# A two-layer transformer stack on one core: in the first feed-forward layer, half a plain column block moves to right behind the first pair's last product

## The chip, the cores and the metric

The kernel runs on one core of one Trainium2 chip. The metric is the time of one execution on the device in microseconds (us), here the median of several runs. Engines are called TensorE (PE), VectorE (DVE), ScalarE (ACT), GpSimd (POOL) and SyncE (SP).

## What is computed

256 tokens of width 1024 go through one layer of a first model (feed-forward, mixer of neighbourhood attention and pooling, feed-forward, a gated embedding) and two layers of a second model (feed-forward, mixer, feed-forward each). The change touches only the very first feed-forward layer, `f1`:

```python
D_MODEL = 1024; SEQ = 256; D_FF = 2816

def rms_norm(x, g):
    xf = x.astype(jnp.float32)
    y = xf * lax.rsqrt(jnp.mean(xf * xf, axis=-1, keepdims=True) + RMS_EPS)
    return (y * g.astype(jnp.float32)).astype(x.dtype)

def swiglu(x, w_gate, w_up, w_down):
    return (jax.nn.silu(x @ w_gate) * (x @ w_up)) @ w_down
...
        f = swiglu(rms_norm(h, ffn1_pre_g[i]), ffn1_w_gate[i], ffn1_w_up[i], ffn1_w_down[i])
        h = h + 0.5 * rms_norm(f, ffn1_post_g[i])
```

## The kernel before

**Tiles.** All products are float32-accurate and are made of three fp32r products: high part of the tokens with high part of the weight, low with high, high with low. A weight tile is 512 rows (four blocks of 128) by 512 columns, 1 MB, and comes in one DMA into a buffer `wholeN`. ScalarE copies it into a buffer `splitM` in fp32r (the **high part**, line 1554, counted by `act_hi`), and VectorE subtracts (the **low part**, line 2029, counted by `dve_lo`, written to `splitN`, over the place of the raw tile). TensorE then runs 12 matmuls of 512 columns for each of the two token tiles `t` = 0, 1: four with the high part (line 892), four with the tokens' low part (line 896), four with the weight's low part (line 905).

**Plain blocks and pairs.** The gate and up projections have 11 column blocks (256 gate columns and the 256 up columns beside them). Blocks 0 to 4, 9 and 10 of `f1` are **plain**: `("tile", j, n)` is block j with rows n of 0, 1, 24 matmuls for both token tiles, into `bank0` and `bank1` or `bank2` and `bank3`. Blocks (5, 6) and (7, 8) are **pairs**: instead of eight block products (two column blocks, two halves of the rows, two token tiles) there are seven, of 12 matmuls each (lines 954, 956, 959), on sums of weights and of tokens, as in Strassen's scheme: `b11`, `t1`, `t2`, `b22`, `t3`, `b21`, `t4`. They share `bank6` and `bank7`, and ScalarE and VectorE carry results between them in the working tiles `u1`, `u2`, `s5`, `c4`, which all lie in `xn`. For a second pair (`g` = 1):

- `b11` goes to `bank6` and must wait until the first pair's `t4` has been read out of it: ScalarE's gate (line 1690) and then VectorE's multiplication (line 2303, the wait on `mult` of the pair's first block).
- ScalarE then copies `bank6` to `u1` (line 1713). This copy waits for `turn 5`, since `turn 5` still reads the old `u1`. Product `t2`, which accumulates into `bank6`, waits for that copy (`fn.of("u1", name, g)`).
- The raw weights of `t1` and `t3` are sums that GpSimd makes with an accumulating DMA (line 704) on top of a first load. Those of `t2` and `t4` are sums that VectorE makes (line 2033): `t2` from `b22` and `t1`; `t4` from `b21` and `t2`.

**Turns.** `("turn", j)` is four transposes on TensorE (line 842) of a finished block of the hidden layer; ScalarE takes the high part (line 1559, `th`), VectorE the low part (line 2076, `tl`).

**What sets the order.** One table, `LATE_PAIRS` (lines 27 to 39), lists tiles, turns and products. Every engine's program for `f1` walks this table, and the number of a weight tile in the plan (`spot`) is its place in it. SyncE issues the loads in the order of `load_key`, which follows the plan's number, with the weights of `t1` pulled to just ahead of `b11`. ScalarE and VectorE also work ahead. At a table's step with weight i, before what else the step asks of it, ScalarE makes the high parts of all weights up to `ahead(i, 1)`, in order, and VectorE the low parts up to `behind(i)`:

```python
        def ahead(i, gap=2):
            j = i
            while j + 1 < NT and j < i + 5 and needed[j + 1] <= i - gap:
                j += 1
            return j
        def behind(i):
            return max(i, ahead(i, 1) - 1)
                elif step == "product":
                    act_high(act, ahead(spot[(name, *what)], 1))
                    product(*what)
```

`needed[j]` is the last weight whose buffers tile j takes over. Each engine works strictly in its own order, so whatever stands behind a waiting instruction waits too. The plan before numbers the weights around the change: 18 is `t4` of the first pair, 19 `b11` of the second, 20 `tile 10, 0`, 21 `t1`, 22 `t2`, 23 `tile 10, 1`, 24 `b22`, 25 `t3`, 26 `b21`, 27 `t4`.

Of the kernel before, what the change touches and what calls it, by code (L numbers as in the profile page):

```python
# [31 lines left out]
    ("product", 0, "b11"), ("tile", 4, 1),  # L32
    ("product", 0, "t1"), ("product", 0, "t2"), ("tile", 9, 0), ("turn", 4),
    ("product", 0, "b22"), ("product", 0, "t3"), ("tile", 9, 1),
    ("product", 0, "b21"), ("product", 0, "t4"), ("turn", 6),
    ("product", 1, "b11"), ("turn", 5), ("tile", 10, 0),
    ("product", 1, "t1"), ("product", 1, "t2"), ("tile", 10, 1),
    ("product", 1, "b22"), ("product", 1, "t3"), ("turn", 9),
    ("product", 1, "b21"), ("turn", 10), ("product", 1, "t4"))
# [2828 lines left out]
```

## Time and profile before

| | us |
|---|---|
| median of 3 runs | 1577.14 |
| lowest, highest | 1576.97, 1578.09 |
| the profiled execution, whole time | 1576.5 |
| its span in the trace | 1574.7 |
| TensorE busy | 1564.3 (99% of the span) |
| VectorE busy | 1225.4 (78%) |
| ScalarE busy | 919.2 (58%) |

The profiled execution is 0.6 us shorter than the median and 1.8 us longer than its own span. TensorE is busy nearly all of the time, so the time is TensorE's work plus the few places where it waits. The changed stretch lies between 93 and 114 us from the span's start, in the third of the profile's 40 slices.

### The profile page before, as it was taken

How to read it: one execution, taken by the hardware profiler on the slowest of the kernel's cores; microseconds unless marked ns; L12 is line 12 of the kernel's file. 1: busy time of each engine (PE TensorE's matmuls, PEld its weight loads, DVE VectorE, ACT ScalarE, POOL GpSimd, SP SyncE). 2: the span in 40 equal slices, each digit the busy share in tenths (PEclk: the TensorE clock that was granted, in tenths of full speed). 3: DMA queues.
4: the chain of work that ended last, by engine and by line, in shares of the span. 5: the costliest groups of instructions: out<-in, count | busy, mean ns of one | idle time of the engine just before them, and what ended most of it. 6: DMA issues, size and time to landing. Idle time of an engine off the chain costs nothing.

```text
span 1574.7 us, 18788 instructions
## 1 busy us (share of the span) xinstructions
PE 1564.3 (99%) x7587; PEld 1303.4 (83%) x7587; DVE 1225.4 (78%) x1168; ACT 919.2 (58%) x957; POOL 116.9 (7%) x138
## 2 busy tenths in 40 slices
PE   9999999999999999999999999999999999999998
PEld 6878897788888888888988888888888998888886
DVE  6888466677889779888658898878897657688887
ACT  7556456656675776654655575466654435455752
POOL 1115000000000000001010000000000131000000
PEclk9999999999999999999999999999999999999999
DMA  9896464467876687674648777868775544576773
GB/s 347 263 272 240 161 237 144 147 244 225 273 247 233 236 285 256 213 242 181 241 161 293 211 244 218 325 209 290 241 267 206 191 170 149 194 279 210 255 219 134
DMA packets 54484, 360.25 MB, mean 229 GB/s; under 512 B 6528, under 2 KB 6912, under 8 KB 13696
## 3 DMA queue, kind: packets, MB, share of 16 engines
q1 hardware_dynamic: 44864, 308.24, 52.0%
q0 software_dynamic: 9312, 50.70, 14.5%
q8 instruction: 60, 0.98, 0.3%
q14 instruction: 24, 0.20, 0.0%
q10 hardware_dynamic: 224, 0.14, 0.0%
HBM read 358.00 MB, written 1.05 MB: 228 GB/s over the span
## 4 chain that ended last, share of the span: by engine, by line
PE 98%; DVE 1%; DMA 0%; issue 0%; ACT 0%; SPq 0%; DVEq 0%; ACTq 0%
PE bank L892 22%; PE bank L905 22%; PE bank L896 19%; PE bank L959 7%; PE bank L954 7%; PE bank L956 7%; PE bank L842 3%; PE bank L909 3%; PE bank L988 2%; PE bank L990 2%; PE bank L991 2%; DVE split L2029 0%; DMA whole<-in_w_f_gate_up 0%; PE bank L1436 0%; PE bank L1226 0%; DVE whole L2033 0%
## 5 line engine op out<-in xcount | busy, mean ns | idle before, releaser
L2029 DVE TENSOR_TENSOR split<-whole,split 128x2048 fp32r<-128x2048 f32 (+2 forms) x346 | 741.8, 2168 | 113.5 <-ACT split L1554 112.6
L1554 ACT ACTIVATE split<-whole 128x2048 fp32r<-128x2048 f32 (+1 forms) x331 | 615.6, 1879 | 235.1 <-DVE whole L2033 59.8
L892 PE MATMUL bank<-split,xh 128*128 128x512 f32 x1020 | 279.6, 396 | 0.0
L905 PE MATMUL bank<-split,xh 128*128 128x512 f32 x1020 | 273.6, 390 | 0.0
L896 PE MATMUL bank<-split,xl 128*128 128x512 f32 x848 | 227.2, 390 | 0.0
L905 PEld LDWEIGHTS bank<-split,xh 128*128 128x128 f32 x1020 | 191.1, 188 | 40.8 <-DVE split L2029 0.6
L892 PEld LDWEIGHTS bank<-split,xh 128*128 128x128 f32 x1020 | 186.8, 188 | 39.4 <-issue 3.0
L896 PEld LDWEIGHTS bank<-split,xl 128*128 128x128 f32 x848 | 159.2, 188 | 34.2
L892 PE MATMUL bank<-split,th 128*128 128x512 f32 x364 | 101.0, 394 | 0.0
L896 PE MATMUL bank<-split,tl 128*128 128x512 f32 x364 | 99.4, 389 | 0.0
L905 PE MATMUL bank<-split,th 128*128 128x512 f32 x364 | 99.4, 389 | 0.0
L896 PEld LDWEIGHTS bank<-split,tl 128*128 128x128 f32 x364 | 68.3, 188 | 14.4
L905 PEld LDWEIGHTS bank<-split,th 128*128 128x128 f32 x364 | 68.3, 188 | 14.4
L892 PEld LDWEIGHTS bank<-split,th 128*128 128x128 f32 x364 | 67.1, 188 | 13.0
L2033 DVE TENSOR_TENSOR whole<-whole 128x2048 f32<-128x2048 f32 x34 | 77.6, 2284 | 0.0
L988 PE MATMUL bank<-xh,split 128*128 128x256 f32 x256 | 72.6, 284 | 0.0
L990 PE MATMUL bank<-xl,split 128*128 128x256 f32 x256 | 72.4, 283 | 0.0
L991 PE MATMUL bank<-xh,split 128*128 128x256 f32 x256 | 72.4, 283 | 0.0
L954 PE MATMUL bank<-split,xh 128*128 128x512 f32 x224 | 61.4, 396 | 0.6 <-DVE xn L2303 0.6
L2076 DVE TENSOR_TENSOR tl<-bank,th 128x512 fp32r<-128x512 f32 x66 | 45.4, 687 | 20.8 <-ACT th L1559 20.2
L956 PE MATMUL bank<-split,xl 128*128 128x512 f32 x224 | 60.0, 390 | 0.0
L959 PE MATMUL bank<-split,xh 128*128 128x512 f32 x224 | 60.0, 390 | 0.0
(335 smaller groups left out, 1998.5 us busy)
## 6 DMA issues: line engine op xcount, KB each, us to landing
whole<-in_w_a_gate_up SPq DMA_DIRECT2D x48, 1024.0 KB, 6.9
whole<-in_w_b_gate_up SPq DMA_DIRECT2D x48, 1024.0 KB, 6.9
whole<-in_w_f_gate_up SPq DMA_DIRECT2D x46, 1024.0 KB, 8.2
whole<-in_w_ret SPq DMA_DIRECT2D x24, 1024.0 KB, 4.8
whole<-in_w_a_down SPq DMA_DIRECT2D x22, 1024.0 KB, 6.8
whole<-in_w_b_down SPq DMA_DIRECT2D x22, 1024.0 KB, 6.8
whole<-in_w_f_down SPq DMA_DIRECT2D x21, 1024.0 KB, 4.9
whole<-in_w_mix SPq DMA_DIRECT2D x16, 1024.0 KB, 4.9
```

What stands on the lines that cost most here:

```text
L892: pe.matmul(o[:, :], tokens(0, k), whi[:, k, :], start=start and k == 0, stop=False, skip_group_check=True)
L896: pe.matmul(o[:, :], tokens(1, k), whi[:, k, :], start=False, stop=False, skip_group_check=True)
L905: ins = pe.matmul(o[:, :], tokens(0, k), wlo[:, k, :], start=False, stop=end, skip_group_check=True)
L954: pe.matmul(o[:, :], xh_of(k), whi[:, k, :], start=start and k == 0, stop=False, skip_group_check=True)
L956: pe.matmul(o[:, :], xl_of(k), whi[:, k, :], start=False, stop=False, skip_group_check=True)
L959: ins = pe.matmul(o[:, :], xh_of(k), wlo[:, k, :], start=False, stop=k == 3, skip_group_check=True)
L988: pe.matmul(o, whi[:, k, cols], xh[:, k0 + k, :], start=start and k == 0 and c % 2 == 0, stop=False, skip_group_check=True)
L990: pe.matmul(o, whi[:, k, cols], xl[:, k0 + k, :], start=False, stop=False, skip_group_check=True)
L991: ins = pe.matmul(o, wlo[:, k, cols], xh[:, k0 + k, :], start=False, stop=end, skip_group_check=True)
L1554: act.activation(split[s][:, 0:n], whole[r][:, 0:n], ACT.Copy).then_inc(hi.mark(i), 1)
L2029: dve.tensor_tensor(split[r][:, c0:c1], whole[r][:, c0:c1], split[s][:, c0:c1].bitcast(F32), ALU.subtract).then_inc(lo.mark(*what), 1)
L2033: dve.tensor_tensor(whole[load_to[i]][:, :], whole[load_to[a]][:, :], whole[load_to[b]][:, :], ALU.add).then_inc(vec.mark("sum", i), 1)
```

## The change

One entry of the table moves: `tile 10, 0` (block 10 with the first half of the rows) stood behind `turn 5`, and now stands right behind the first pair's `t4`, ahead of `turn 6`. The second pair's `b11`, `turn 5` and `t1` now follow each other directly.

```diff
     ("product", 0, "b22"), ("product", 0, "t3"), ("tile", 9, 1),
-    ("product", 0, "b21"), ("product", 0, "t4"), ("turn", 6),
-    ("product", 1, "b11"), ("turn", 5), ("tile", 10, 0),
+    ("product", 0, "b21"), ("product", 0, "t4"), ("tile", 10, 0), ("turn", 6),
+    ("product", 1, "b11"), ("turn", 5),
     ("product", 1, "t1"), ("product", 1, "t2"), ("tile", 10, 1),
```

`tile 10, 0` becomes weight 19 and `b11` weight 20. No instruction is added or removed; buffers are dealt out anew from weight 17 to 29.

**TensorE**, from the first pair's `t4` (the first row) to the second pair's `t1` (the last row, with `sh`). Before:

```order
L959 MATMUL bank<-split,xh 128x512 x4
L842 MATMUL bank<-ident,xn 128x128 x4
L954 MATMUL bank<-split,xh 128x512 x4
L956 MATMUL bank<-split,xl 128x512 x4
L959 MATMUL bank<-split,xh 128x512 x4
L842 MATMUL bank<-ident,xn 128x128 x4
L892 MATMUL bank<-split,xh 128x512 x4
L896 MATMUL bank<-split,xl 128x512 x4
L905 MATMUL bank<-split,xh 128x512 x4
L892 MATMUL bank<-split,xh 128x512 x4
L896 MATMUL bank<-split,xl 128x512 x4
L905 MATMUL bank<-split,xh 128x512 x4
```

Now, from the first matmuls of `tile 10, 0` on:

```order
L892 MATMUL bank<-split,xh 128x512 x4
L896 MATMUL bank<-split,xl 128x512 x4
L905 MATMUL bank<-split,xh 128x512 x4
L842 MATMUL bank<-ident,xn 128x128 x4
L954 MATMUL bank<-split,xh 128x512 x4
L956 MATMUL bank<-split,xl 128x512 x4
L959 MATMUL bank<-split,xh 128x512 x4
L842 MATMUL bank<-ident,xn 128x128 x4
L954 MATMUL bank<-split,sh 128x512 x4
```

The 24 matmuls of lines 892 to 905 moved from behind the second turn to ahead of the first.

**ScalarE**, the same place. Line 1690 is the gate of the first pair's `t4`, `th0<-bank5` is `turn 6`, `th0<-bank4` is `turn 5`, line 1713 is the copy to `u1`; of line 1554, the one that waits for `dma_sum_t1` is weight 21 (`t1`), the one with `dve_vec` is 22 (`t2`), the one with `dma_raw9` is 23 (`tile 10, 1`). Before:

```order
L1690 ACTIVATE xn<-bank6,st 128x256 [waits pe_passed]
L1559 ACTIVATE th0<-bank5 128x512 [waits pe_turned]
L1554 ACTIVATE split8<-whole4 128x2048 [waits pe_passed,dma_sum_t1]
L1713 ACTIVATE xn<-bank6 128x512 [waits pe_turned,pe_passed]
L1559 ACTIVATE th0<-bank4 128x512 [waits pe_turned]
L1554 ACTIVATE split6<-whole0 128x2048 [waits pe_passed,dve_vec]
L1554 ACTIVATE split5<-whole9 128x2048 [waits pe_passed,dma_raw9]
```

Now:

```order
L1690 ACTIVATE xn<-bank6,st 128x256 [waits pe_passed]
L1554 ACTIVATE split4<-whole5 128x2048 [waits pe_passed,dma_sum_t1]
L1559 ACTIVATE th0<-bank5 128x512 [waits pe_turned]
L1554 ACTIVATE split6<-whole0 128x2048 [waits pe_passed,dve_vec]
L1554 ACTIVATE split8<-whole9 128x2048 [waits pe_passed,dma_raw9]
L1713 ACTIVATE xn<-bank6 128x512 [waits pe_turned,pe_passed]
L1559 ACTIVATE th0<-bank4 128x512 [waits pe_turned]
```

The copy to `u1` (line 1713) stood ahead of the high parts of 22 and 23, and stands behind them now: at its step, `b11`, the rule `ahead(i, 1)` now gives 23, where it gave 21.

**VectorE**, the same place. `tl0<-bank5` is `turn 6`, `tl0<-bank4` is `turn 5`, line 2033 makes the weight sums of `t2` and `t4`; the rows of line 2029 behind them are the low parts of `t1` and `t2`. Before:

```order
L2076 TENSOR_TENSOR tl0<-bank5,th0 128x512 [waits act_turn_hi]
L2029 TENSOR_TENSOR split1<-whole1,split3 128x2048 [waits act_hi]
L2076 TENSOR_TENSOR tl0<-bank4,th0 128x512 [waits act_turn_hi]
L2033 TENSOR_TENSOR whole0<-whole10,whole4 128x2048 [waits dma_sum_t1,dma_raw10,pe_passed]
L2029 TENSOR_TENSOR split4<-whole4,split8 128x2048 [waits act_hi]
L2033 TENSOR_TENSOR whole2<-whole11,whole0 128x2048 [waits dve_vec,dma_raw11,pe_passed]
L2029 TENSOR_TENSOR split0<-whole0,split6 128x2048 [waits act_hi]
```

Now:

```order
L2029 TENSOR_TENSOR split1<-whole1,split3 128x2048 [waits act_hi]
L2076 TENSOR_TENSOR tl0<-bank5,th0 128x512 [waits act_turn_hi]
L2033 TENSOR_TENSOR whole0<-whole10,whole5 128x2048 [waits dma_sum_t1,dma_raw10,pe_passed]
L2029 TENSOR_TENSOR split5<-whole5,split4 128x2048 [waits act_hi]
L2033 TENSOR_TENSOR whole2<-whole11,whole0 128x2048 [waits dve_vec,dma_raw11,pe_passed]
L2029 TENSOR_TENSOR split0<-whole0,split6 128x2048 [waits act_hi]
L2076 TENSOR_TENSOR tl0<-bank4,th0 128x512 [waits act_turn_hi]
```

The chain of weight sums and low parts stood behind `turn 5` and stands behind `turn 6` now.

SyncE's loads keep their number and places; only what the first of them bring is exchanged: the load that follows the first pair's `t2` brings weight 19 (`tile 10, 0`) where it brought the first part of 21 (`t1`), the load behind `tile 9, 0` brings 21 where it brought `b11`, and the load behind `b22` brings `b11` where it brought `tile 10, 0`.

## Rows read from the trace of the kernel before

**Rows 1.** The profile's page, part 1: busy time of each engine.

```profile
PE 1564.3 (99%) x7587; PEld 1303.4 (83%) x7587; DVE 1225.4 (78%) x1168; ACT 919.2 (58%) x957; POOL 116.9 (7%) x138
```

**Rows 2.** TensorE's waits, whole span: for whom, us in total, times, longest.

```profile
PE bank L959 <- DVE split L2029: 0.7, 1, 0.7
```

**Rows 3.** TensorE in order of time, 94 to 114 us: start, us, what, idle before it.

```profile
96.50 0.60 PE L842 MATMUL bank<-ident,xn 128*128 128x128 f32 x4
97.75 1.19 PE L954 MATMUL bank<-split,xh 128*128 128x512 f32 x4 [0.65 <-DVE xn L2303]
...
100.61 0.60 PE L842 MATMUL bank<-ident,xn 128*128 128x128 f32 x4
100.96 1.18 PE L892 MATMUL bank<-split,xh 128*128 128x512 f32 x4
...
106.53 1.07 PE L954 MATMUL bank<-split,sh 128*128 128x512 f32 x4
...
109.25 1.07 PE L954 MATMUL bank<-split,sh 128*128 128x512 f32 x4
...
111.97 1.20 PE L959 MATMUL bank<-split,sh 128*128 128x512 f32 x4 [0.74 <-DVE split L2029]
113.01 1.08 PE L892 MATMUL bank<-split,xh 128*128 128x512 f32 x4
```

**Rows 4.** ScalarE in order of time, the same stretch.

```profile
97.78 1.92 ACT L1554 ACTIVATE split<-whole 128x2048 fp32r<-128x2048 f32 x1
101.30 0.60 ACT L1713 ACTIVATE xn<-bank 128x512 f32<-128x512 f32 x1 [1.61 <-PE bank L842]
101.80 0.59 ACT L1559 ACTIVATE th<-bank 128x512 fp32r<-128x512 f32 x1
105.35 1.92 ACT L1554 ACTIVATE split<-whole 128x2048 fp32r<-128x2048 f32 x1 [2.96 <-DVE whole L2033]
109.96 3.72 ACT L1554 ACTIVATE split<-whole 128x2048 fp32r<-128x2048 f32 x2 [2.69 <-DMA whole<-in_w_f_gate_up]
```

**Rows 5.** VectorE in order of time, the same stretch.

```profile
102.42 0.69 DVE L2076 TENSOR_TENSOR tl<-bank,th 128x512 fp32r<-128x512 f32 x1 [1.76 <-ACT th L1559]
103.03 2.28 DVE L2033 TENSOR_TENSOR whole<-whole 128x2048 f32<-128x2048 f32 x1
105.23 2.29 DVE L2029 TENSOR_TENSOR split<-whole,split 128x2048 fp32r<-128x2048 f32 x1
107.43 2.28 DVE L2033 TENSOR_TENSOR whole<-whole 128x2048 f32<-128x2048 f32 x1
109.63 6.77 DVE L2029 TENSOR_TENSOR split<-whole,split 128x2048 fp32r<-128x2048 f32 x3
```

**Rows 6.** Line 650, SyncE's weight loads, 93 to 95 us: issue, issue to landing.

```profile
L650 SPq DMA_DIRECT2D whole<-in_w_f_gate_up x1: 328/328/328, 94.0 to 94.0; - x1
...
DMA to landing us min/median/max: 16.0/16.0/16.0
```

**Rows 7.** The same line, 79 to 81 us.

```profile
L650 SPq DMA_DIRECT2D whole<-in_w_f_gate_up x1: 328/328/328, 79.9 to 79.9; - x1
...
DMA to landing us min/median/max: 6.3/6.3/6.3
```

**Rows 8.** Line 704, GpSimd's accumulating load, 83 to 84 us.

```profile
L704 POOL DMA_DIRECT2D whole<-in_w_f_gate_up x1: 983/983/983, 83.4 to 83.4; - x1
...
DMA to landing us min/median/max: 14.3/14.3/14.3
```

**Rows 9.** Stretches: us, busy PE, PEld, DVE, ACT, POOL, clock, DMA share, GB/s.

```profile
94.00:106.00 12.00, 11.35 (x54) 9.21 (x53) 10.16 (x9) 5.20 (x7) 1.37 (x2) 1.00 1.03 331
```

**Rows 10.** DMA packets, 89 to 96 us: packets, MB, share of 16 engines.

```profile
q0 software_dynamic: 128, 0.99, 67.9%
q1 hardware_dynamic: 132, 0.95, 34.2%
```

**Rows 11.** TensorE's first matmuls of the span.

```profile
1.20 3.53 PE L1514 MATMUL bank<-junk 128*128 128x512 bf16 x8 [1.20 <-DVE eps L2721]
```

## The prediction

> **What bounds the kernel now.** I read the page first: TensorE is busy 1564.3 of 1574.7 us [rows 1], so only its work and its few waits set the end. No work is added or taken away here, so I looked at its waits. Outside the kernel's first 7 us, the view of waits has two, and both lie in the changed stretch: one for a weight's low part [rows 2] and one for VectorE's multiplication, which stands as idle time in the order of time [rows 3]. I then read the three engines in order of time over that stretch [rows 3 to 5], and last the DMAs that feed it [rows 6 to 10].
>
> The reader is to see two things in rows 3. Four matmuls of 512 columns take 0.907 us, since the 12 of `t1` take from 106.53 to 109.25, 2.72 us. And two steps take longer. (a) `turn 6` starts at 96.50 and its successor `b11` at 97.75, 1.25 us where `turn 5` and its successor need 0.35 (100.61 to 100.96): 0.90 us lost, waiting for the first pair's last multiplication. (b) `t2` takes 3.76 us (109.25 to 113.01) where 2.72 are due: 1.04 us lost, waiting for its low part. Together 1.94 us, 0.12% of the time. This is all that the move can give back.
>
> **The change, part by part: TensorE.** `t4` ends at 96.50, and nothing up to there is touched on TensorE. `tile 10, 0` now starts there. Its high part is made where ScalarE made that of `b11`, its low part likewise; both are older than 96.50 or end before it is needed. Cost 24 matmuls, 6 x 0.907 = 5.44 us, to 101.94, as before but earlier. The wait (a) goes: the multiplication was done at 97.7. Then `turn 6` 0.35, `b11` 2.72, plus 0.13 that the first matmuls behind a turn always cost (97.75 to 100.61 is 2.86 [rows 3]): 105.14. `turn 5` 0.35 brings `t1` to 105.49, where before it stood at 106.53. So far the gain is 1.04 us.
>
> **The change: VectorE.** Its chain (sum for `t2`, low part of `t1`, sum for `t4`, low part of `t2`; 2.2 us each) started at 103.03, right behind `turn 5`'s low part, for which it had waited on ScalarE [rows 5]. Now it stands behind `turn 6`, and that turn starts at 101.94. From `turn 5` at 100.61 [rows 3] to the chain at 103.03 were 2.42 us, of which ScalarE's copy to `u1` held up nothing more than 0.50 (101.30 to 101.80 [rows 4]). Without that copy the chain starts at 101.94 + 1.92 = 103.86, so 0.83 later than before, for products that TensorE wants 1.04 earlier. The low part of `t1` ends at 107.43 + 0.83 = 108.26. TensorE wants it at 105.49 + 0.13 + 1.81 = 107.43, gets it at about 108.4, and ends `t1` at 109.44. The low part of `t2` ended at 111.83 (109.63 + 2.2) and ends at 112.66.
>
> **The change: ScalarE, the step that decides.** The copy to `u1` (line 1713) ran at 101.30 [rows 4] as soon as `turn 5` was through, eight us before `t2` needed it. Now ahead of it stand the high parts of weights 22 and 23. That of 22 waits for VectorE's sum and ended at 107.15; it shifts with the chain to 108.0. That of 23 (`tile 10, 1`) waits for a load which was issued at 94.0 and took 16.0 us [rows 6]: ScalarE began it at 109.96 after 2.69 us of waiting for that DMA [rows 4]. Before, this load hid behind `t1`, `t2` and the stall of `t2`. Now `t2` hangs on it: 109.96, plus 1.80 until ScalarE can start the next (two take 3.72, one 1.92 [rows 4]), plus 0.60 for the copy, gives 112.4 as the start of `t2`. TensorE has been free since 109.44, so it waits 3.0 us. By then everything else that `t2` needs is there or nearly so: its low part, at 112.7, is wanted at 112.4 + 1.9 = 114.3. So `t2` ends at 112.4 + 2.86 = 115.26, where it ended at 113.01 [rows 3].
>
> **Sum.** At the end of `t2` the same work is done in both orders, so the difference there is the whole effect: 115.26 - 113.01 = +2.25 us. Written as terms: -0.90 (wait a) - 1.04 (wait b) + 1.1 (new wait of `t1` with its restart) + 3.0 + 0.1 (new wait of `t2`) = +2.3. Behind it both lists are the same, and each part has more room than before: the low part of `tile 10, 1` is now behind `turn 5`'s low part and ends near 116.0, wanted at 117.2. I find no later wait of TensorE that could absorb the loss [rows 2]. Profiled execution 1576.5 + 2.25 = 1578.75; the median was 0.6 above the profiled execution: **1579.4 us**.
>
> **The DMAs.** SyncE's loads leave at the same moments; only three exchange contents. The base of the sum for `t1` now comes with the load issued at 79.9, landing at 86.2 [rows 7], so GpSimd can issue the accumulating load only then, where it did at 83.4 [rows 8]. With the same 14.3 us [rows 8] it lands at 100.5, not 97.7. ScalarE's high part of `t1` then runs to 102.4 and just clears `turn 6` at 102.6; up to about 1.4 us more would still leave `t2` where it is, since its low part has that much room. Does the later accumulation move the landing of weight 23? The DMA engines are full from 94 to 106 us (share 1.03 [rows 9]), and what has to be moved by 110 is the same, so I take 109.96 as it stands. The bounds: earlier than 107 it no longer decides; at worst it is late by the 2.8 us that the accumulation starts later.
>
> The page "DMA: Bandwidth & Descriptors" of the Trainium skill, section "Queues, rings and completion order", says that a DMA engine takes turns between its queues packet by packet. Rows 10 agree: 128 software packets and 132 hardware packets in 7 us. By that rule the late accumulation can steal turns from weight 23; that is rival 2. What it would do here by rows: an accumulating packet costs the engines twice a plain one (67.9% of their time for 128, against 34.2% for 132 [rows 10]), so a load that shares its time with the accumulation goes at a third of the rate.
>
> **Rivals.**
> 1. The load is not what `t2` waits for (weight 23 lands by 107, or the copy is not held). Then only VectorE's chain is left: `t2`'s low part at 112.8 with restart ends it at 113.84, +0.8 us: 1578.0. For it: landings here run from 6.3 to 16.0 us [rows 6, 7]. Against: the engines are full [rows 9].
> 2. Weight 23 lands later, by up to 2.8 us. Each us costs one: up to +5.05 us, 1582.2. It would be slower by more than 0.2% from 0.9 us of delay on.
> 3. The clock of TensorE. With `t1` split by a wait and then 3.0 us of nothing, TensorE is idle for 4.0 of 5 us. The first eight matmuls of the span, after idleness, took 3.53 us, 0.44 each [rows 11], against 0.227 in the stretch: the lower of its two levels (1.2 against 2.4 GHz). If that happens once more behind the wait, eight matmuls lose 8 x 0.213 = 1.7 us: +3.95, 1581.1, slower. It decides if the wait reaches what the gate takes for idleness; the waits shown here, under 1 us, did not trigger it [rows 2, 3], so the trace bears it out only at the start. The Trainium skill, "TensorE: Matmul & The Clock Gate", section "HAM oscillation — how this bites in real kernels", says that long gaps send the array back to the half rate; no row here shows a gap of this size.
> 4. The move does what it seems made for: both waits go and none comes. 1577.14 - 1.94 = 1575.2, within 0.2% still. It needs VectorE's low part of `t2` by 110.2, 2.4 us before the chain can end. I see no way.
>
> **How the numbers follow.** Forecast 0.66, with its own range of 1578.6 to 1580.2 (half a us and some either way for the landing and the latencies); rival 1 0.12; rival 2 0.07; rival 3 0.12; rival 4 0.03. The measurement tells about 0.2% (3.15 us) from no change: below 1574.0 is faster, above 1580.3 slower. Forecast, rivals 1 and 4 are "same" (0.81), less a little of the forecast's upper edge; rival 3 and most of rival 2 are slower: 0.19. Nothing but an unseen effect is faster: 0.02. The forecast and rival 1 hold only 0.78, so the range takes in rival 3 as well: 1577.4 to 1581.4.
>
> **What would show it.** In the changed profile: TensorE without the wait at 97; a wait of some 0.8 us inside `t1` for line 2029; a wait of some 3 us ahead of `t2` (line 954, tile `sh`) put down to ScalarE's line 1713; ScalarE's line 1554 just ahead of that copy waiting for the DMA until about 110; `t2` followed by line 892 at 115.3. If the matmuls behind the wait take 0.44 us each, rival 3 holds; if the view shows a wait for line 2029 ahead of 113 and none for line 1713, rival 1. The prediction is wrong if the landing of weight 23 moves, or if another load that I took as early enough (the accumulation for `t1`) lands behind 102.

## The result and the profile after

The changed kernel takes 1580.7 us (median of 9 runs, 1578.70 to 1583.77), the kernel before 1577.14 us (9 runs, 1576.82 to 1578.13). The ratio is 1.0024 with a 95% interval of 1.0013 to 1.0034: slower by 0.24%, 3.6 us. The profiled execution took 1580.7 us with a span of 1578.9.

TensorE's view of waits, over the whole span, has two rows in the changed stretch: one new, and one that answers to [rows 2].

```profile
PE bank L954 <- ACT xn L1713: 2.2, 1, 2.2
...
PE bank L959 <- DVE split L2029: 0.8, 1, 0.8
```

TensorE in order of time, answering to [rows 3] (start, us, what, idle before it):

```profile
97.98 1.07 PE L892 MATMUL bank<-split,xh 128*128 128x512 f32 x4
...
103.42 0.60 PE L842 MATMUL bank<-ident,xn 128*128 128x128 f32 x4
103.78 1.17 PE L954 MATMUL bank<-split,xh 128*128 128x512 f32 x4
...
109.83 1.20 PE L959 MATMUL bank<-split,sh 128*128 128x512 f32 x4 [0.77 <-DVE split L2029]
113.19 1.27 PE L954 MATMUL bank<-split,sh 128*128 128x512 f32 x4 [2.15 <-ACT xn L1713]
114.25 1.91 PE L956 MATMUL bank<-split,sl 128*128 128x512 f32 x4
115.96 1.83 PE L959 MATMUL bank<-split,sh 128*128 128x512 f32 x4
117.63 1.07 PE L892 MATMUL bank<-split,xh 128*128 128x512 f32 x4
```

The first row is `tile 10, 0`, which starts as `t4` ends, at 97.98 (96.50 in the profile of before: this execution lost 1.48 us in its first microseconds, waiting for the inputs). Then come `turn 6`, `b11` without a wait, `turn 5`, `t1` with a wait inside, and a wait of 2.15 us ahead of `t2`. And something that has no counterpart before: the twelve matmuls of `t2` take from 113.19 to 117.63, 4.44 us, where 2.86 are due behind a pause. The last two groups of four start 1.71 and 1.67 us ahead of what follows them (0.907 elsewhere): these eight ran at the lower level of the clock, and the view by stretches says so (columns as in [rows 9]: behind the busy times of the five engines come the granted clock, the DMA share and GB/s):

```profile
110.00:114.00 4.00, 1.84 (x8) 1.19 (x9) 4.00 (x2) 3.26 (x4) 0.71 (x1) 1.00 0.97 201
114.00:118.00 4.00, 4.00 (x12) 3.14 (x11) 4.00 (x4) 3.44 (x3) 0.00 (x0) 0.57 0.45 164
118.00:122.00 4.00, 4.00 (x20) 3.30 (x19) 4.00 (x3) 4.00 (x4) 0.00 (x0) 1.00 0.40 131
```

ScalarE in order of time, answering to [rows 4]:

```profile
99.75 1.92 ACT L1554 ACTIVATE split<-whole 128x2048 fp32r<-128x2048 f32 x1 [1.09 <-DMA whole<-in_w_f_gate_up]
...
107.61 1.92 ACT L1554 ACTIVATE split<-whole 128x2048 fp32r<-128x2048 f32 x1 [2.96 <-DVE whole L2033]
110.74 1.91 ACT L1554 ACTIVATE split<-whole 128x2048 fp32r<-128x2048 f32 x1 [1.21 <-DMA whole<-in_w_f_gate_up]
112.56 0.58 ACT L1713 ACTIVATE xn<-bank 128x512 f32<-128x512 f32 x1
```

The row at 110.74 is the high part of weight 23, which waited for its load until 110.74; the copy to `u1` stands right behind it, ends at 113.14, and releases `t2` at 113.19. The load itself, answering to [rows 6]:

```profile
L650 SPq DMA_DIRECT2D whole<-in_w_f_gate_up x1: 327/327/327, 95.5 to 95.5; - x1
...
DMA to landing us min/median/max: 15.3/15.3/15.3
```

**The account.** I measure the stretch from the end of `t4` to the end of `t2`, within which both orders do the same work: 113.01 - 96.50 = 16.51 us before [rows 3], 117.63 - 97.98 = 19.65 us after, +3.14. The spans differ by 4.2 us: 1.48 at the start, 3.14 here, -0.4 in all the rest. The start is not the change's: up to `t4` TensorE does the same, and in the profiles below `t4` ends anywhere from 96.5 to 99.8. The medians differ by 3.6 us, 0.4 more than the stretch; what makes up that 0.4 is not shown.

### The profile page after: what moved, and what is told of

It is laid out like the page before. It is cut to its first block, busy times and chain, and to the rows that moved or that the text cites. A ratio compares the mean times of both kernels' runs of the same rounds, so it can differ in the third digit from the quotient of the medians.

```text
span 1578.9 us, 18788 instructions
## 1 busy us (share of the span) xinstructions
PE 1565.9 (99%) x7587; PEld 1304.7 (83%) x7587; DVE 1225.3 (78%) x1168; ACT 919.1 (58%) x957; POOL 116.6 (7%) x138
## 4 chain that ended last, share of the span: by engine, by line
PE 98%; DMA 1%; DVE 0%; issue 0%; SPq 0%; ACT 0%; DVEq 0%; ACTq 0%
PE bank L892 22%; PE bank L905 22%; PE bank L896 19%; PE bank L956 7%; PE bank L954 7%; PE bank L959 7%; PE bank L842 3%; PE bank L909 3%; PE bank L988 2%; PE bank L990 2%; PE bank L991 2%; DMA whole<-in_w_f_gate_up 1%; DMA h<-in_x 0%; PE bank L1436 0%; PE bank L1226 0%; PE bank L1245 0%
```

## The experiments

Each was timed in five rounds beside the kernel before on the same chip. "Stretch" is the same piece of the profile, from the end of `t4` to the end of `t2`; before it is 16.51 us. The theory: the copy to `u1` waits behind the load of weight 23, and the pause that this opens lets TensorE's clock fall. The rivals: VectorE's chain, which also came later; the loads that exchanged contents; and a slow clock that is chance, or has another cause than the pause.

### The changed kernel again

No edit.

> The changed kernel once more, as the measure for the three beside it on the same chip. Its profile showed two costs in one place: TensorE stood 2.2 us ahead of t2 for ScalarE's copy to u1, and then ran the twelve matmuls of t2 in 4.4 us instead of 2.9, at a granted clock of 0.57 in 114 to 118 us. If both belong to the change and not to that one execution, the median is again 3 to 4 us over the kernel before (1580 to 1581) and the profile has a t2 of over 4 us. If the slow clock was a chance of one execution, the median comes out at the +2.3 us of the waits alone (1579.4).

1580.84 us (1578.20 to 1582.75, 11 runs) against 1577.19 (33 runs), ratio 1.0020 [1.0011, 1.0029]. Its stretch is 20.26 us, and the slow matmuls are there again:

```profile
113.50 1.92 PE L954 MATMUL bank<-split,sh 128*128 128x512 f32 x4 [2.76 <-ACT xn L1713]
115.22 1.91 PE L956 MATMUL bank<-split,sl 128*128 128x512 f32 x4
116.93 1.18 PE L959 MATMUL bank<-split,sh 128*128 128x512 f32 x4
```

So both costs belong to the change. The slow clock was no accident of one execution.

### The copy ahead of the load

```diff
                 elif step == "product":
-                    act_high(act, ahead(spot[(name, *what)], 1))
+                    if name == "f1" and what == [1, "b11"]:
+                        act_high(act, grp[1].t1)
+                    else:
+                        act_high(act, ahead(spot[(name, *what)], 1))
                     product(*what)
```

> The changed order, but ScalarE makes the high parts at step b11 of the second pair only up to weight 21, so that the copy to u1 stands ahead of the high parts of 22 and 23, as in the kernel before. Theory (the copy queued behind the load of weight 23 is the cause, and the slow clock follows from that wait): t2 is left with the later chain of VectorE alone, the wait is under 1.2 us, the clock stays up, and the time is +0.8 us on the kernel before, 1577.9. Rival (it is the position of VectorE's chain, or the loads that exchanged contents): the time stays near 1580. Rival (the slow clock comes from the split t1 or from something else in the place): the wait goes, the slow matmuls stay, about 1579.5.

1578.01 us against 1577.19, ratio 1.0006 [0.9997, 1.0014]; stretch 17.29 us, +0.78. TensorE around `t2`:

```profile
110.18 1.07 PE L954 MATMUL bank<-split,sh 128*128 128x512 f32 x4
111.09 1.07 PE L956 MATMUL bank<-split,sl 128*128 128x512 f32 x4
113.55 1.19 PE L959 MATMUL bank<-split,sh 128*128 128x512 f32 x4 [1.39 <-DVE split L2032]
```

The wait for the copy is gone, the clock stays up, and what is left is VectorE's later chain: 0.77 us inside `t1` and 1.39 inside `t2`. The theory's 0.8 us came out; the rival by which the chain or the loads alone carry the loss is out. One size was off: I had expected under 1.2 us for the single wait.

### The pause filled

```diff
                 elif m == "t2":
+                    if name == "f1" and g == 1:
+                        pe.wait_ge(vec.sem, vec.of("mult", name, 9, 1))
+                        for _ in range(9):
+                            pe.matmul(bank[2][:, :], junk[:, 0:P], junk[:, 0:512], start=True, stop=True,
+                                      skip_group_check=True)
                     pe.wait_ge(fn.sem, fn.of("u1", name, g))
```

> The changed order with nine idle matmuls (bf16, 512 columns, into bank2, which nobody uses then; their result is never read) on TensorE ahead of t2, about 2.0 us of the gap of 2.3 us. The wait for the copy to u1 ends at the same moment as before. Theory (the gap lets the clock fall): the clock stays up, t2 takes 2.9 us again, and the time is 1.5 us less than the changed kernel's, about 1579.1. Rival (the slow clock is not caused by the gap, or the loss is all wait): no difference to the changed kernel, 1580.7. Where the copy comes early, the filling itself costs a few tenths.

The matmuls go to `bank2`, and nobody reads what they write; the first wait holds them until that bank is free. 1579.11 us against 1577.19, ratio 1.0012 [1.0003, 1.0021], and 1.7 us less than the changed kernel on the same chip (the means of their 11 runs each differ by 1.6 us, three times the standard error). The stretch is 114.55 - 96.53 = 18.02 us, +1.51. TensorE:

```profile
109.65 1.89 PE L1068 MATMUL bank<-junk 128*128 128x512 bf16 x8
111.70 1.20 PE L954 MATMUL bank<-split,sh 128*128 128x512 f32 x4 [0.16 <-ACT xn L1718]
112.74 1.07 PE L956 MATMUL bank<-split,sl 128*128 128x512 f32 x4
...
114.55 1.07 PE L892 MATMUL bank<-split,xh 128*128 128x512 f32 x4
```

`t2` starts 15.17 us behind the end of `t4`, as late as in the changed kernel (15.21), but takes 2.85 us. Work without any use made the kernel faster: the pause is what lets the clock fall, and that part costs about 1.6 us.

### The copy behind the load, in the order of before

```diff
+                    if g and name == "f1" and not late:
+                        return
...
                         act_high(act, ahead(spot[name, j, n], 1))
+                    if name == "f1" and (j, n) == (10, 0):
+                        product(1, "b11", True)
```

(`late` is a new argument of ScalarE's `product`; it is false at the step `b11`, where the copy stood, and true in the added call.)

> The order of the kernel before, with one part of the change alone: ScalarE's copy to u1 stands behind the high parts of weights 22 and 23 (turn 5's high part stays where it was). VectorE's chain, the loads and TensorE's order are those of the kernel before. Theory (the position of the copy is enough): t2 starts at about 112.4 instead of 109.25 and waits 3.1 us, which swallows the wait for its low part: +2.3 us, and with the clock falling behind the gap 1.6 more: 1580.9 (1579.4 if the clock holds). Rival (the change's other parts are needed, the chain or the loads): within 0.5 us of 1577.1.

1580.33 us against 1577.19, ratio 1.0019 [1.0010, 1.0028]. TensorE's order, the loads and VectorE are those of before, and this one displaced copy costs 3.1 us. Stretch 118.56 - 99.80 = 18.76 us, +2.25:

```profile
115.71 1.19 PE L954 MATMUL bank<-split,sh 128*128 128x512 f32 x4 [3.00 <-ACT xn L1715]
116.74 1.08 PE L956 MATMUL bank<-split,sl 128*128 128x512 f32 x4
...
118.56 1.07 PE L892 MATMUL bank<-split,xh 128*128 128x512 f32 x4
```

In this execution the clock held through the pause of 3.0 us. It had fallen once already, at the kernel's start, behind a wait for the first input:

```profile
10.78 0.66 PE L842 MATMUL bank<-ident,h 128*128 128x128 f32 x4 [1.84 <-DMA h<-in_x]
...
13.05 1.91 PE L892 MATMUL bank<-split,xh 128*128 128x512 f32 x4
```

That fall is not the edit's, and it is part of why `t4` ends at 99.80 here. So the mean clock of a run (0.998 in this one) does not say where in the kernel the clock fell. The median is 0.9 us over what the stretch explains, and four of the 11 runs have a mean clock of 0.997, which none of the 89 runs of before in these comparisons has. That fits a clock that falls behind the copy in some executions and not in others. No profile of this kernel shows it, so it stays an inference.

### VectorE's chain ahead of the turn, copy left where the change put it

```diff
                 elif step == "turn":
+                    if name == "f1" and what == [6]:
+                        dve_lows(dve, grp[1].t2)
                     turn(*what)
```

> The changed order, ScalarE as in it (the copy to u1 behind the high parts of 22 and 23), but VectorE makes the weight sums and low parts up to weight 22 ahead of turn 6's low part instead of behind it. Theory (the copy alone sets the start of t2): the wait of 0.8 us inside t1 goes, t1 ends 1.1 us earlier, the wait ahead of t2 grows by the same 1.1 us to over 3 us, and the time stays that of the changed kernel, 1580.8, or a little more if the longer gap costs more clock. Rival (VectorE's chain carries part of the loss): 1 us less, 1579.8.

1580.95 us (7 runs) against 1576.98, ratio 1.0026 [1.0015, 1.0037]; stretch 19.89 us. As the theory has it: the wait inside `t1` is gone, and the one ahead of `t2` has grown.

```profile
112.56 1.46 PE L954 MATMUL bank<-split,sh 128*128 128x512 f32 x4 [3.43 <-ACT xn L1713]
113.82 1.91 PE L956 MATMUL bank<-split,sl 128*128 128x512 f32 x4
115.53 1.65 PE L959 MATMUL bank<-split,sh 128*128 128x512 f32 x4
```

The clock fell here too (1.71 us for the four of line 956), and behind a single pause: no wait of TensorE stands ahead of it in this stretch.

### The same in the order of before

The edit is the one above with `[5]` for `[6]`, in the kernel before.

> The order of the kernel before with VectorE's chain (sum for t2, low part of t1, sum for t4, low part of t2) ahead of turn 5's low part instead of behind it. It touches only wait (b) of the prediction, 1.04 us. Theory (the chain was late because it stood behind a turn): the wait inside t2 goes, wait (a) of 0.65 us stays, 1576.1. Rival (something behind it, a load or ScalarE's high part, ends late too): less than 0.5 us gained.

1577.60 us against 1576.98, ratio 1.0003 [0.9994, 1.0012]: nothing gained, the theory missed. The wait inside `t2` did go, but ScalarE's rows show what came next (the first is the high part of weight 22, the second those of 23 and 24, the third that of the sum for `t3`):

```profile
103.83 1.92 ACT L1554 ACTIVATE split<-whole 128x2048 fp32r<-128x2048 f32 x1 [0.51 <-DVE whole L2033]
111.12 3.72 ACT L1554 ACTIVATE split<-whole 128x2048 fp32r<-128x2048 f32 x2 [5.37 <-DMA whole<-in_w_f_gate_up]
116.95 1.92 ACT L1554 ACTIVATE split<-whole 128x2048 fp32r<-128x2048 f32 x1 [2.11 <-DMA whole<-in_w_f_gate_up]
```

ScalarE waited 5.4 us for the load of weight 23. `tile 10, 1` got its high part 0.17 us late and its low part 0.22 us late. `b22` started late too, since the copy that it needs (line 1718) stands behind the third row: once more a short copy behind a high part that waits for a load. From the end of `t4` to `turn 9` are 27.53 us, where before they are 27.42: what `t2` won is lost behind it, to weights that landed late.

### The move with both repairs

The edit of the second experiment with `grp[1].t2` for `grp[1].t1`, and that of the fifth.

> The changed order with both repairs: ScalarE's copy to u1 ahead of the high part of weight 23 (behind that of 22), and VectorE's chain ahead of turn 6's low part. Theory (the move was worth its 1.94 us, and the two queues it was moved past took it away): no wait of TensorE is left between 90 and 130 us, and the time is 1575.2, the fastest of all. Rival (the accumulating load for t1, issued later by the exchange of the loads, holds the chain): the wait for the low part of t2 is still there, 1576 to 1577. If the first repair alone gave 1578.0, the second is worth 2.8 us here.

1576.98 us against 1576.98, ratio 1.0003 [0.9994, 1.0012]. The changed kernel stood 3.7 us over the kernel before; this one is no slower than before, but no faster either. One of its 11 runs took 1583.19 us with a mean clock of 0.997; where it lost that is not shown. TensorE's view of waits:

```profile
PE bank L892 <- ACT split L1554: 1.1, 1, 1.1
...
PE bank L905 <- DVE split L2032: 0.2, 1, 0.2
```

The time won up to the end of `t2` is lost again at `tile 10, 1`, whose high part hangs on the same load of weight 23 (ScalarE starts it 13.90 us behind `t4`), and at `b22`, as in the run before this one. From the end of `t4` to `turn 9` are 27.81 us.

### The bias loads out of the way

GpSimd issues 16 loads of the mixer's bias in small packets while these weights are on their way, and its two accumulating loads for the second pair stood among the last eight of them. They are wanted only by the mixer, behind this layer.

```diff
+            pool_sum(pool, "t1", group["f1", 1].t1)
+            pool_sum(pool, "t3", group["f1", 1].t3)
             for n in range(8):
-                if n == 3:
-                    pool_sum(pool, "t1", group["f1", 1].t1)
-                if n == 7:
-                    pool_sum(pool, "t3", group["f1", 1].t3)
                 pool.wait_ge(lo.sem, lo.of(14 + n))
```

In the changed kernel:

> The changed kernel, with one thing moved on GpSimd alone: its two accumulating loads for the second pair are issued ahead of the second eight bias loads (small packets, wanted only by the mixer), not among them. That takes the bias loads out of the full DMA queues of 82 to 110 us. Theory (the copy to u1, and with it t2, waits for the landing of weight 23): that load lands about 2 us earlier (107 to 108.5 by the profile of before's clock), the wait ahead of t2 shrinks by as much to under 1 us, the clock stays up, and the time falls from 1580.8 to 1578.3. Rival (what the copy waits for is not bound to the DMA traffic): 1580.8 again.

1578.05 us against 1577.30 (33 runs), ratio 1.0004 [0.9995, 1.0013]. The profiled execution is the slowest of the 11 (1580.66): its clock fell at the start, behind a wait of 1.63 us for the input, before anything of the change. Only its stretch is used here: 116.98 - 99.67 = 17.31 us, +0.80. TensorE and ScalarE (all line numbers are two lower in this kernel):

```profile
111.53 1.20 PE L957 MATMUL bank<-split,sh 128*128 128x512 f32 x4 [0.77 <-DVE split L2027]
113.56 1.21 PE L952 MATMUL bank<-split,sh 128*128 128x512 f32 x4 [0.83 <-ACT xn L1711]
...
115.93 1.21 PE L957 MATMUL bank<-split,sh 128*128 128x512 f32 x4 [0.24 <-DVE split L2027]
```

```profile
109.30 3.72 ACT L1552 ACTIVATE split<-whole 128x2048 fp32r<-128x2048 f32 x2 [2.96 <-DVE whole L2031]
112.92 0.58 ACT L1711 ACTIVATE xn<-bank 128x512 f32<-128x512 f32 x1
```

The high parts of 22 and 23 now follow each other without a wait for the DMA, the copy comes behind them, and the pause is 0.83 us. The load of weight 23:

```profile
L650 SPq DMA_DIRECT2D whole<-in_w_f_gate_up x1: 328/328/328, 97.1 to 97.1; - x1
...
DMA to landing us min/median/max: 9.6/9.6/9.6
```

It took 9.6 us instead of 15.3, so it landed nearly 6 us earlier, not the 2 that I had expected, and no longer sets the copy's start: that is now the high part of 22. Nothing on TensorE, ScalarE or VectorE was reordered. In the changed kernel seven of the eight bias loads left between 79.9 and 101.7 us; here all eight leave behind 105. The accumulating loads wait for their base loads in both kernels: the first leaves at the same place (11.0 and 11.3 us ahead of the end of `t4`), the second earlier (4.9 us behind it instead of 8.6), because its base landed earlier too. So the bias loads are what the edit took away from in front of weight 23. It is worth 2.9 us (0.75 over the kernel before instead of 3.65).

With both repairs:

> The changed order with both repairs (copy to u1 ahead of the high part of weight 23, VectorE's chain ahead of turn 6's low part) and the bias loads out of the way as well. The run with both repairs alone gained nothing: TensorE then waited 1.1 us for the high part of weight 23 and 0.2 us for its low part, and started b22 late. Theory (the loads of 23 and of t3 are the floor under this stretch): with them earlier no wait is left and the 1.9 us come: 1575.2. Rival (bias loads cost too little): 1576 to 1577.

1575.01 us (1574.25 to 1576.37, 11 runs) against 1577.30, ratio 0.9985 [0.9976, 0.9994]: faster than both kernels. The stretch is 111.83 - 97.27 = 14.56 us, 1.95 less than before, and TensorE waits nowhere in it. Its view of waits has only the kernel's start:

```profile
PE bank L1512 <- DVE eps L2724: 1.2, 1, 1.2
PE bank L840 <- DMA h<-in_x: 1.1, 1, 1.1
```

In the kernel before:

> The kernel before with the bias loads out of the way, as the measure for the other three. Its two waits (for the last multiplication, and for VectorE's chain) do not depend on the DMA. Theory: no change, 1577.1. Rival (the DMA sets the pace here already): 0.5 us or more gained.

1576.73 us, ratio 0.9998 [0.9989, 1.0007]: no difference that can be measured. The medians differ by 0.6 us, so the rival's 0.5 us isn't excluded either.

In the kernel before with VectorE's chain ahead of `turn 5`:

> The kernel before with VectorE's chain ahead of turn 5's low part and the bias loads out of the way; the moved tile stays where it was. With the bias loads in the way the chain alone gained nothing, since TensorE met the landing of weight 23 and of the sum for t3 right behind. Theory: the wait of t2 (1.04 us) is now gained, wait (a) of 0.9 us stays: 1576.1; the difference to the run with the moved tile, both repairs and light loads is what the move itself is worth, 0.9 us. Rival: no gain, 1577.1.

1575.90 us, ratio 0.9993 [0.9984, 1.0002]. The median is 0.2 us from the theory's. The intervals of this kernel and of the one with the moved tile overlap where both are taken against the kernel before. Taken against each other, on the same chip, the medians differ by 0.9 us and the means by 0.7, three times the standard error; and from the end of `t4` to `turn 9` this one takes 26.35 us, the other 25.45. This one still has the wait of 0.6 us for the last multiplication, the other has none. So the move itself is worth about 0.9 us.

## Why the prediction was right, and where not

The range (1577.4 to 1581.4) held the time. The forecast of 1579.4 was 1.3 us too low, and the likeliest case was not the whole story: what happened is rival 3, the forecast's wait with a fallen clock behind it, to which I had given 0.12. That its 1581.1 is only 0.4 off is in part luck: it has the stretch 0.8 us too long, and the medians hold 0.4 us that the stretch does not. My 0.79 for "within 0.2%" went against a result of 0.24%.

- **Wait (a) goes, -0.90.** Right: `turn 6` at 103.42, `b11` at 103.78.
- **VectorE's chain 0.83 later; a wait inside `t1` of 0.8 us.** Right: 0.77 us. The run with the copy ahead of the load shows the chain alone as +0.78 in the stretch; the changed kernel with light loads, where the last wait of `t2` is again for its low part, has +0.80.
- **The copy behind the load of weight 23.** Right, and confirmed from three sides: putting the copy ahead of the load removes the wait, putting it behind in the old order makes one of 3.0 us and a stretch of +2.25, and an earlier landing shortens it.
- **Start of `t2`, 15.9 us behind `t4`.** 15.2 us. The high part of 23 started 12.76 us behind the end of `t4` instead of 13.46, so the pause was 2.15 us instead of 3.0. I had taken the landing from a single execution; in the profiles in which ScalarE waits for it, it lies between 12.7 and 13.9 us. I had also left the bias loads out of the account of the DMAs: with these moved it came nearly 6 us earlier.
- **`t2` itself, 2.86 us.** The term that was mis-sized: 4.44 us, since the clock fell. Sum of the stretch: 2.25 - 0.69 + 1.58 = 3.14 us. The mechanism stood among the rivals with about the right price (1.7 us), but with too small a chance, on the ground that waits under 1 us did no harm. Such rows say nothing of one two to three times as long. The Trainium skill, "TensorE: Matmul & The Clock Gate", section "HAM oscillation — how this bites in real kernels", says that long gaps send the array back to the half rate. Both profiles of the changed kernel agree, with matmuls of 0.43 us behind pauses of 2.15 and 2.76 us; the gaps of the page's example are longer than these.
- **No later wait that absorbs the loss.** Right: from the end of `t4` to `turn 9` the changed kernel takes 30.54 us against 27.42, +3.12, so behind `t2` nothing was won or lost.
- **The accumulating load.** Right: issued when its base had landed (87.0), landed 12.7 us later (I had taken 14.3), and ScalarE's next step was still in time for `turn 6` (99.75 + 1.92 against 104.06).
- **"This is all that the move can give back", 1.94 us.** Right as a sum, wrong as a price within reach. I had ruled rival 4 out on account of VectorE's chain alone. Moving the copy and the chain gave nothing against the kernel before, because weight 23 was the next bound, which I had not carried on past `t2`. Only with the bias loads moved too did the stretch get the 1.95 us back.

## What to carry to other kernels

When a step is moved in a shared table, list for each in-order engine what a work-ahead rule now pulls in front of the small steps that TensorE waits for; here a rule that looked five tiles ahead put a wait for a load in front of a 0.6 us copy, and gave back more than the move removed. A pause of TensorE like those seen here (1.6 to 3.4 us, all but the longest close behind shorter ones) should be priced with a fallen clock, as a case of its own weight and not as an afterthought, and with the spread of the landings that set it. And before the repair of a wait is priced, look for the next bound behind it: here a load in a full DMA queue, which moving other, less urgent loads made earlier.

## What the runs showed of the hardware

- The granted clock of TensorE fell to 0.57 in a 4 us stretch (110 to 114: 1.00, 118 to 122: 1.00) behind a pause of 2.15 us that followed a wait of 0.77 us; matmuls of 512 columns took 0.43 us from start to start (1.71 for four, 114.25 to 115.96), which is its lower level, 1.2 GHz. Of two profiles with a single pause, the one of 3.43 us (VectorE's chain ahead of the turn) shows the fall, and the one of 3.0 us (the copy displaced in the old order) shows the upper level, 2.4 GHz.
- The same fall came at the kernel's start, where TensorE waits for the input: in the two profiles with the longest such wait (1.84 and 1.63 us, close behind shorter ones) the granted clock was 0.83 over 10 to 20 us. In the eight profiles that show this wait with 0.17 to 1.24 us it was 1.00. So the time of one execution also depends on when its first input lands.
- Nine useless matmuls in the pause kept the clock up and saved 1.7 us of the whole.
- A weight load of 1 MB took 15.3 us from issue to landing where seven loads of 128 KB in small packets had been issued from 16 us ahead of it on, and 9.6 us where these were issued 8 us behind it and later.
- The changed kernel's runs scatter more: a standard deviation of 1.4 us over 11 runs, where the 33 of the kernel before beside it have 0.7. With both repairs and light loads it is 0.6. A stretch that hangs on a landing and on the clock is not only slower but less steady.
